# The shift and scale vectors of a conditioned decoder layer summed along the free axis on VectorE instead of through accumulators and column-of-ones matmuls

## The reference, cut to what matters

```python
c_act = jax.nn.silu(c)
mod = c_act @ w_ada[l] + b_ada[l]
sh1, sc1, g1, sh2, sc2, g2 = jnp.split(mod, 6, axis=-1)
h = rmsnorm(x, norm1_g[l]) * (1.0 + sc1[:, None]) + sh1[:, None]
proj = h @ w_in[l]                      # 1024 -> 3072 columns
...                                     # 4 differential heads, 8 MoBA heads, shared bias table
x = x + g1[:, None] * mix               # mix = [A | B] @ w_out
h2 = rmsnorm(x, norm2_g[l]) * (1.0 + sc2[:, None]) + sh2[:, None]
x = x + g2[:, None] * peer(h2, ...)     # 16384 single-neuron experts, 8 heads, top 16
return rmsnorm(x, final_g)
```

## Time and profile before

| | |
|---|---|
| median of 3 runs | 1034.99 us (1034.63 to 1036.53) |
| the profiled execution's own time | 1034.67 us |
| span of the profiled execution | 1032.9 us |
| granted clock of TensorE, mean | 0.973 |
| PE busy | 960.8 us (93%) |
| DVE busy | 740.6 us (72%) |
| ACT busy | 486.9 us (47%) |
| POOL busy | 278.7 us (27%) |
| DMA | 191.60 MB, mean 186 GB/s |

### The profile page before, as it was taken

One profiled execution on the slowest core, in us unless ns is written; L12 is line 12 of the kernel. 1 busy time (PEld: TensorE's weight loads), 2 busy tenths in 40 slices (PEclk: granted clock), 3 DMA queues, 4 the chain that ended last, 5 costly groups with the idle time before them and its releaser, 6 DMA issues.

```text
span 1032.9 us, 16975 instructions
## 1 busy us (share of the span) xinstructions
PE 960.8 (93%) x6674; PEld 881.5 (85%) x6674; DVE 740.6 (72%) x1358; ACT 486.9 (47%) x865; POOL 278.7 (27%) x138
## 2 busy tenths in 40 slices
PE   2299898699999999999999999999999999999996
PEld 2198778698999999999999999988888888888884
DVE  4935869870699998789999998555555555555555
ACT  5355435332644454454444444454545454545453
POOL 5566446656799995000000000000000000000000
PEclk9599999899999999999999999999999999999998
DMA  9994457612365665554545545666666666666662
GB/s 291 285 363 168 164 202 328 265 62 103 102 184 165 183 184 165 164 160 149 163 149 158 156 152 164 184 183 195 193 195 193 195 192 193 194 193 195 193 194 102
DMA packets 58162, 191.60 MB, mean 186 GB/s; under 512 B 4946, under 2 KB 23522, under 8 KB 56932
## 3 DMA queue, kind: packets, MB, share of 16 engines
q1 hardware_dynamic: 58018, 190.50, 57.3%
q0 software_dynamic: 64, 0.03, 0.0%
q10 hardware_dynamic: 2, 0.00, 0.0%
HBM read 189.44 MB, written 1.07 MB: 184 GB/s over the span
## 4 chain that ended last, share of the span: by engine, by line
PE 82%; DVE 9%; POOL 4%; ACT 2%; issue 1%; DMA 1%; SPq 0%; DVEq 0%; ACTq 0%
PE banks L899 22%; PE banks L906 11%; PE banks L875 11%; PE banks L879 11%; PE banks L876 10%; PE banks L720 5%; DVE acc L962 5%; POOL lo L434 4%; PE banks L890 3%; PE banks L729 2%; PE banks L717 1%; DMA sc_w<-in_w_ada 1%; PE banks L726 1%; DVE prob L1085 1%; PE banks L857 1%
## 5 line engine op out<-in xcount | busy, mean ns | idle before, releaser
L1231 DVE TENSOR_TENSOR lo<-raw,hi 128x1024 fp32r<-128x1024 f32 x210 | 258.9, 1233 | 169.7 <-ACT hi L591 168.3
L591 ACT ACTIVATE hi<-raw 128x1024 fp32r<-128x1024 f32 x256 | 271.5, 1061 | 169.7 <-PE banks L906 169.7
L875 PE MATMUL banks<-h2r,hi 128*128 128x256 f32 x1024 | 256.4, 288 | 0.0
L899 PE MATMUL banks<-hi,wsplit 128*128 128x512 f32 x1024 | 253.2, 389 | 0.5 <-DVE wsplit L1272 0.5
L876 PE MATMUL banks<-h2r,hi 128*128 128x256 f32 x1024 | 251.1, 283 | 0.0
L899 PEld LDWEIGHTS banks<-hi,wsplit 128*128 128x128 f32 x1024 | 192.2, 188 | 40.5 <-issue 0.7
L876 PEld LDWEIGHTS banks<-h2r,hi 128*128 128x128 f32 x1024 | 196.6, 192 | 0.0
L875 PEld LDWEIGHTS banks<-h2r,hi 128*128 128x128 f32 x1024 | 196.0, 191 | 0.0
L879 PE MATMUL banks<-h2r,lo 128*128 128x256 f32 x1024 | 143.9, 283 | 3.4 <-POOL lo L434 3.4
L906 PE MATMUL banks<-lo,wsplit 128*128 128x512 f32 x512 | 137.0, 389 | 0.0
L879 PEld LDWEIGHTS banks<-h2r,lo 128*128 128x128 f32 x1024 | 132.0, 192 | 4.2 <-POOL lo L434 4.2
(11 more groups left out here) (171 smaller groups left out, 1057.8 us busy)
## 6 DMA issues: line engine op xcount, KB each, us to landing
raw<-in_u_t SPq DMA_DIRECT2D x128, 512.0 KB, 3.6
raw<-in_v_b SPq DMA_DIRECT2D x128, 512.0 KB, 3.8
win<-in_w_in SPq DMA_DIRECT2D x8, 1024.0 KB, 11.9
g_w<-in_w_ada SPq DMA_DIRECT2D x2, 4096.0 KB, 14.3
wq<-in_wq SPq DMA_DIRECT2D x2, 4096.0 KB, 13.7
sh_w<-in_w_ada SPq DMA_DIRECT2D x4, 1024.0 KB, 11.9
sc_w<-in_w_ada SPq DMA_DIRECT2D x4, 1024.0 KB, 12.1
win<-in_w_in SPq DMA_DIRECT2D x1, 4096.0 KB, 19.1
```

Of the source, the lines that this page charges most:

```text
L591: nc.scalar.activation(hi_t[:, n % HI, :], raw[n % RAW][:, :], ACT.Copy).then_inc(high_ready, 1)
L875: nc.tensor.matmul(dst, w, h2r[:, 0, c, :], start=(c == 0), stop=False)
L899: nc.tensor.matmul(bank[2 * t + half][:, :], wsplit[:, j % WS, e, t * P:(t + 1) * P], hi_t[:, n % HI, half * 512:half * 512 + 512], start= ...
L1231: nc.vector.tensor_tensor(lo_t[n % RAW][:, :], raw[n % RAW][:, :], hi_t[:, n % HI, :].bitcast(F32), ALU.subtract).then_inc(vector_low, 1)
```

## The change

The weights of `sh1`, `sc1`, `sh2` and `sc2` are laid out the other way round by the host: output feature on the partitions, input features along the free axis. `c` is loaded once more, as a row repeated on all partitions (`crow`), and ACT applies Silu to it. One DVE instruction per 128 output features, a tensor_tensor_reduce over 1024 elements, then multiplies by `crow`, sums, starts from the bias and writes one column of the vector; it is followed by an instruction that reads the accumulator out. The column-of-ones matmuls, the tree on POOL, the products on ACT and the bias additions of `modulate` are gone. The first stage's loads are five pieces for each vector (2, 2, 2, 1 and 1 chunks of 128 output features). `g1` and `g2` are made as before, but their bias rows are loaded repeated on all partitions into `g1b` and `g2b` by SP, and DVE adds them to the matmul's result in place of PE's second matmul.

```diff
-            for e in range(PARTS):
-                c = slice(e * GW, (e + 1) * GW)
-                for n, (dst, src) in ((1, (sh1_w, w_ada[0])), (0, (sc1_w, w_ada[1]))):
-                    sp.dma_start(dst[:, :, c], src[:, :, c]).then_inc(part_in[n][e], 16)
+            for e, (lo, hi) in enumerate(PIECES):
+                sp.dma_start(sh1_w[:, lo:hi, :], w_mod[0][:, lo:hi, :]).then_inc(shift_in[e], 16)
+                sp.dma_start(sc1_w[:, lo:hi, :], w_mod[1][:, lo:hi, :]).then_inc(scale_in[e], 16)
...
+            sp.dma_start(g1b[:, :], b_row[0:1, :].broadcast_to([P, D])).then_inc(g1row_in, 16)
+            sp.dma_start(g2b[:, :], b_row[1:2, :].broadcast_to([P, D])).then_inc(g2row_in, 16)
...
+            def mod_chunk(w, a, kind, col, c):
+
+                return nc.vector.tensor_tensor_reduce(out=w[:, c, :], in0=w[:, c, :], in1=crow[:, :], scale=1.0,
+                                                      scalar=bcol[:, col, c:c + 1], op0=ALU.mult, op1=ALU.add,
+                                                      accum_out=a[:, kind, c:c + 1])
...
             def ada(k, chunks):
...
-                    add_chunk(dst, ada_w[ADA[k]], c, acc_ready)
+                    if k in (0, 3):
+                        add_chunk(acc if k == 0 else acc_g2, ada_w[ADA[k]], c, acc_ready)
+                    else:
+                        ins = mod_chunk(ada_w[ADA[k]], a2, k - 1, k + 1, c)
...
-            sc.wait_ge(cact_ready, 1)
-            shift_products(0)
-            shift_products(1)
             for b in range(DC // 2):
-                if b + 2 < PARTS:
-                    shift_products(b + 2)
-                if b == 2:
+                if b == DC // 2 - 1:
                     high_group(0)
                 high_columns(hh, a1, b, b + 1, place_h, xT_ready, hT_even, hT_odd, h_high)
...
+            def mod_row(src, half, dst):
+
+                return nc.tensor.matmul(dst, ones[:, :], src[:, half * 512:half * 512 + 512], start=True, stop=True)
...
-            mod_column(1, 0, (0, 1))
-            mod_column(2, DC // 2, (0, 1))
...
-            def row_copy(n, src, dst):
+            def row_add(n, src, dst):
                 ve.wait_ge(rows_ready, n)
-                nc.vector.tensor_copy(dst, src).then_inc(rows_read, 1)
+                ve.wait_ge(g1row_in, 16)
+                nc.vector.tensor_tensor(dst, src, dst, ALU.add).then_inc(rows_read, 1)
...
-            nc.vector.tensor_scalar(g2b[:, :], banks[:, 0:2, :].rearrange("p b n -> p (b n)"), 1.0 / GATE_SCALE,
-                                    None, ALU.mult).then_inc(rows_read, 1)
+            link(nc.vector.tensor_tensor(g2b[:, :], banks[:, 0:2, :].rearrange("p b n -> p (b n)"), g2b[:, :], ALU.add))
+            nc.vector.tensor_scalar(g2b[:, :], g2b[:, :], 1.0 / GATE_SCALE, None, ALU.mult).then_inc(rows_read, 1)
```

More of the change, by code:

```diff
@@ L353, in _ @@
             sp.wait_ge(group_done, N_IN)
-            load("sh2", sh2_w, w_ada[3])
+            load("sh2", sh2_w, w_mod[2])
             sp.wait_ge(acc_ready, 2)
@@ L745, in _ @@
             to_columns(xs, xT_ready, range(DC), place_h, scaled=True)
-            for e in range(PARTS):
-                first_columns(e)
             for step in STEPS[:FIRST]:
@@ L843, in _ @@
                     pe.wait_ge(acc_ready, 4)
-                    pe.wait_ge(g2row_in, 16)
                     for half in range(2):
-                        last = mod_row(acc_g2, brow2, half, bank[half])
+                        last = mod_row(acc_g2, half, bank[half])
                     last.then_inc(rows_ready, 1)
@@ L1031, in _, with shift, scale @@
             ve.wait_ge(cact_ready, 1)
-            def first_scale(e):
-                ve.wait_ge(part_in[0][e], 16)
-                cols = slice(e * GW, (e + 1) * GW)
-                for c in range(DC):
-                    add_chunk(acc[:, 1, cols], sc1_w[:, :, cols], c, sc1_ready)
+            def shift(e):
+                ve.wait_ge(shift_in[e], 16)
+                for c in range(*PIECES[e]):
+                    mod_chunk(sh1_w, a1, 1, 1, c).then_inc(sh1_ready, 1)
+            def scale(e):
+                ve.wait_ge(scale_in[e], 16)
+                for c in range(*PIECES[e]):
+                    mod_chunk(sc1_w, a1, 0, 0, c).then_inc(sc1_ready, 1)
             def first_pair(b):
-                modulate(a1, 0, slice(2 * b, 2 * b + 2), bank[4 + b][:, 0:4], b + 1)
+                ve.wait_ge(sc1_ready, 2 * b + 2)
+                modulate(a1, 0, slice(2 * b, 2 * b + 2))
                 odd_chunk(a1, b, b + 1, place_h, xT_ready, hT_odd)
-            first_scale(0)
-            first_scale(1)
-            for b in range(2):
-                first_pair(b)
-                first_scale(b + 2)
-                rest(hh, b, h_high, h_split)
+            ve.wait_ge(small_in, 16)
+            ve.wait_ge(crow_ready, 1)
+            shift(0)
+            scale(0)
+            shift(1)
+            first_pair(0)
+            scale(1)
+            rest(hh, 0, h_high, h_split)
+            shift(2)
+            first_pair(1)
+            scale(2)
+            rest(hh, 1, h_high, h_split)
+            shift(3)
             first_pair(2)
+            scale(3)
+            shift(4)
+            rest(hh, 2, h_high, h_split)
+            scale(4)
             first_pair(3)
-            rest(hh, 2, h_high, h_split)
             rest(hh, 3, h_high, h_split)
@@ L1166, in _ @@
             root(1, 3, TT + TT * N_OUT)
-            for half in range(2):
-                modulate(a2, 1, slice(half * DC // 2, (half + 1) * DC // 2), bank[half][:, 0:DC], PARTS + 3 + half)
+            ve.wait_ge(acc_ready, 3)
+            modulate(a2, 1, slice(0, DC))
             for b in range(DC // 2):
-                odd_chunk(a2, b, PARTS + 1 + b // 2, place_h2, x2T_ready, h2T_odd)
+                odd_chunk(a2, b, PARTS + 1, place_h2, x2T_ready, h2T_odd)
                 if b:
```

110 lines of the change are left out of this document (31 added, 79 removed).

## The result

The changed kernel takes 1025.24 us (median of 4 runs, 1024.02 to 1026.06); the kernel before, run beside it on the same chip, 1035.76 (1034.63 to 1038.09). The ratio is 0.9895 [0.9873, 0.9916]: faster by 10.5 us, where 17.0 was forecast, and 1.2 us above the top of the range. The profiled execution took 1026.06 us, the slowest of its four, with a span of 1024.2. That of the kernel before took 1034.67, near its lowest, with a span of 1032.9. So the traces differ by only 8.7 us.

The account below looks back on a forecast made before the run. PE, busy 93% of the span, was taken as the bound, with DVE's sums leading in stage 1 and the `sh2` block. Gains 12.9 + 4.2 - 0.3 + 0.2 = 17.0 us from 1034.67 gave 1017.7; range 1012.5 to 1024.

Parts of the forecast that it names:

- The price of a reduction, 1.20 us: Stage 1 on DVE: each 1024-column reduction takes 1.20 us from start to start, 16 of them 19.2 us.
- the dearer reduction: Rival, chance 0.14: accumulator read does not overlap, or each reduction costs 1.5 to 1.7 us; total 1023 to 1027 us.
- the half rate: Rival, chance 0.04: two cycles per column, 2.25 us a reduction; slower than before, 1041.3 us.
- The transfer as stage 1's second bound, 38.3 us: Stage 1: the first `win0` load lands at 38.3 us, and this DMA branch ends last, by 1.7 us.
- `high` at 38 to 39 and ending DMA's wait: Expected sign in stage 1: ACT's first `high` comes at 38 to 39 us and ends DMA's wait.
- DVE no longer takes POOL's turns: End of stage 1: POOL's second half and the next group's high part fit; part of the 12.9 us gain.
- with some cold left: PE's first group: after POOL's low half, 0.96 + 1.92 + 0.96 us and some low clock; group ends at 47.1.
- `sc2` is threaded between attention units where PE leads: 0: Attention units: the eight `sc2` reductions replacing sums on DVE cost no time.
- the four gate rows: Gate halves at two places: PE loses four bias-row matmuls of 1.05 us, all in the chain; gain 4.2 us.
- 32 column matmuls of stage 4: 0: Stage 4: the removed column matmuls lay in PE's wait for `diag`, so removing them gains nothing.
- `sh2` takes turns: Stage 3: five or six of eight reductions wait for a turn with POOL, 3.32 us each; costs 0.3 us.
- `g1` does not wait: After stage 1: loading the `g1` weights is hidden, by about 1 us; otherwise 0 to 2 us lost.

Follow-up runs that it names:

- the filling matmuls: Changed kernel plus matmuls nobody reads on PE in stage 1, 14 ahead of the first group and 5 ahead of its last two chunks; 1022.12 us, ratio 0.9873.
- the second profile: The changed kernel run once more with no edit; 1024.70 us, ratio 0.9901.
- the table's trace: The changed kernel's first profiled execution, compared stretch by stretch with the one trace of the kernel before; 1026.06 us.
- the kernels with the fill: Changed kernel plus filling matmuls inside attention, 4 at unit 7 and 2 at unit 15: 1021.79 us; with four other edits too: median 1015.21 from four of six runs.

## Why the prediction was half right

**The price of a reduction, 1.20 us: right.** It ruled out the dearer reduction and the half rate at once. The Trainium skill, Vector Engine (DVE) Microarchitecture Reference, Points that are easy to get wrong, names half throughput for the scalar_tensor_tensor form with two non-bf16 SBUF sources. The reduction is another form with two such sources; the trace shows no halving for it, with 1.28 us for 1024 columns and an accumulator read behind, nor for the sum of that form (1.30).

**The transfer as stage 1's second bound, 38.3 us: wrong, and it opened the next step's fault.** I had priced all at 348 GB/s; from 20 to 25 us the changed kernel moved 414, and SP issued `win0` from 10.8 instead of 24.90. ACT had the weights at 34.88 or sooner, so POOL started at 36.86 and not at 40.2. The forecast had counted the same bytes ahead of `win0` as before. The transfers do fall into fewer packets (58162 before, 51710 after on the pages); whether that made them faster was not tried. The mark "`high` at 38 to 39 and ending DMA's wait" did not show.

**The step that failed: "DVE no longer takes POOL's turns".** It was right that the tree is gone. But the step let POOL's first low parts fit beside a DVE that was done, and because the weights came earlier, DVE was not: one reduction and one modulation were left. They took 2.1 and 2.0 us more than others of their kind. Even at the forecast's own times the step did not hold: it had DVE's last low part at 41.4 to 42.1, beside POOL's first half at 40.2 to 42.7, and with POOL moved back that low part took 1.73 us instead of 0.69. Moving POOL back, by a wait or by a later `high`, took the end of the first group from 49.65 to 52.10 in six profiles to 48.4 and 48.6, and the ratio from 0.9901 to 0.9859 and 0.9863. The rule by which I let them take turns (the Trainium skill, SBUF — State Buffer, Who interferes with whom) agrees with this too; I applied it in stage 3 and not in stage 1.

**The term that was too small: "with some cold left".** From the last input PE waits for to the end of the first group I had 4.4 us (POOL's low half at 42.7, the group at 47.1). From that input, now the last `hh` part at 44.8, it took 7.3, 2.9 of it the low clock (3.35 for 1.92, and 1.22 and 1.71 ahead of it). With the filling matmuls it takes 4.6. These two account for stage 1: 44.8 instead of 42.7, and 7.3 instead of 4.4, together 5.0 of the 12.9; the group ended at 52.1, not 47.1. How much of the clock's part shows differs by execution: in the second profile the group ended at 49.65.

**"`sc2` is threaded between attention units where PE leads: 0": wrong at unit 10.** PE lost the row there and no longer led. Two reductions of 2.4 and 3.3 us ahead of the logits took 1.7 more than the two operations of before, since both now wait for POOL and only the second did: the allowance of 0.3 to 0.5 that I made for this in stage 3 I did not make here. This is the new wait behind the old one, and the stretch fell short of its forecast by 1.6. Putting them behind the logits gave 1.8 back in that stretch and 1.2 in all. That the sum of the four gate rows is 4.2 was right for PE's work (1.2, 1.05, 2.5 with a little for the matmuls behind); 3.1 reached the end.

**"32 column matmuls of stage 4: 0": not shown to be wrong.** They were hidden in a wait, and they shortened PE's idle time from 10.72 to 7.35 us. The 32 transposes behind it took 5.59 us, not the 6.54 of the table's trace, and the stretch 0.5 less. But with the matmuls gone the transposes take 5.50 to 6.54 us and the stretch 23.41 to 24.06 in nine profiles, so one trace of the kernel before, with 5.59 and 23.57, decides nothing. What is shown is that PE kept busy there gives 0.5 to 1.1 us.

**Unit 7: not in the prediction at all.** The 0.6 and 1.4 us lost there in two executions of the changed kernel are not due to any edit at that place. In every kernel PE idles 4 us there and then works at the low clock; when it rises decides the loss. That differs by execution: two profiles of experiments without an edit there took 12.78 and 12.81 us, as the kernel before (12.80), eight took 13.40 to 14.20. Whether the change shifts these odds is open, with one trace of the kernel before. All of them lose some 1.5 us or more against the kernels with the fill.

**Right: `sh2` takes turns (22.0 us against 22.2), `g1` does not wait** (DVE's first `acc` at 97.17 has no idle time ahead), **and what was gained at 60 us stays** through the projections, 51.1 us for the next seven groups in both.

My range of 1012.5 to 1024.0 had rivals for the price of the instruction and for the transfer, and none for the clock or for a DVE chain that takes the lead in stage 2. Of the 8.3 us by which the profiled execution fell short of 17.0, 5.0 are in stage 1 (2.1 turns, 2.9 clock), 1.4 at unit 7, 1.6 at unit 11 and 0.7 in stage 4, less 0.4 at the `g2` row. The clock's part of stage 1, unit 7 and stage 4 are partly this execution's bad luck: the second profile of the same kernel has a span of 1020.6, 3.6 less. The turns and unit 11 are there in both.

## What to carry to other kernels

When an edit moves one engine's work earlier, go through the instructions of each pair that take turns once more at the new times; an operation on two elements per partition can cost 2 us. Where TensorE idles, ask what runs behind the idle time and at which granted clock: matmuls that nobody reads, put into its idle times, were worth 2 to 3 us at two places and 0.5 to 1.1 us at a third. Before explaining a difference between two traces by an edit, look at the same stretch in traces that do not have the edit. And when the leader's work at a place shrinks, add up the runner-up's chain there before booking the gain.

## What the runs showed of the hardware that I had not expected

A VectorE operation on 128x2 elements takes 2.17 us beside GpSimd's subtraction and 0.16 us without it. It ended at 42.78, when GpSimd's second subtraction did (36.86 and 5.91), so it seems to wait for the rest of the other's instruction, whatever its own size. One on 128x1 elements took 2.34 us beside GpSimd, in the run with GpSimd moved back, and 0.15 us in the changed kernel.

TensorE's granted clock fell while TensorE was busy. With the bias rows back it had run 4 us of gate-row matmuls without a gap, weight loads busy only half of that time, and the clock went to 0.81 and 0.62 in the stretches around and behind their end; the 16 matmuls behind took 3.69 us. In the kernel before the same matmuls stood there, with weight loads as little busy (1.40 of 3.00 us in 243 to 246), the clock stayed at 1.00, and the 16 behind took 2.18. What set the two apart is not known from these runs.

The 4 us of idle time at unit 7 cost 1.5 us in matmuls at the low clock even in the kernel before.
